# RWKV stage of a two-block layer stack: products and masks moved from GpSimd to VectorE

## The reference, cut to what matters

```python
r, k, v, gate, wd, ad = split_cols(pf, RWKV_SIZES)
w_log = -jax.nn.softplus(-(w0 + jnp.tanh(wd) @ w_up)) - 0.5
decay = jnp.exp(-jnp.exp(w_log))
a = jax.nn.sigmoid(a0 + ad @ a_up)
kk = k * k_k
k = k * (1.0 + (a - 1.0) * k_a)
kk = kk / jnp.maximum(jnp.sqrt(jnp.sum(kk * kk, axis=-1, keepdims=True)), 1e-12)
def step(S, inp):
    r_t, w_t, k_t, v_t, kk_t, a_t = inp
    sa = jnp.einsum('bhvk,bhk->bhv', S, -kk_t)
    S = (S * w_t[:, :, None, :] + sa[..., None] * (kk_t * a_t)[:, :, None, :]
         + v_t[..., None] * k_t[:, :, None, :])
    y = jnp.einsum('bhvk,bhk->bhv', S, r_t)
    return S, y
# then group norm of y over each head, y + sum(r * k * r_k) * v, times silu(gate)
```

## Time and profile before

| what | us |
|---|---|
| median of three runs (lowest, highest) | 2475.47 (2472.58, 2487.47) |
| the profiled execution | 2476.14 |
| its span, first to last instruction | 2474.3 |
| busy: PE, DVE, ACT, POOL | 2249.0, 840.2, 582.5, 585.7 |

### The profile page before, as it was taken

The page is one execution under the profiler, slowest core; times in us unless marked ns, Lnnn a source line. Parts: engine busy times, 40 slices in busy tenths (PEclk is TensorE's granted clock), DMA queues, the critical chain, the costliest instruction groups (busy, mean ns, idle before and its releaser), DMA issues.

```text
span 2474.3 us, 41370 instructions
## 1 busy us (share of the span) xinstructions
PE 2249.0 (91%) x17921; PEld 1472.3 (60%) x17921; DVE 840.2 (34%) x1741; ACT 582.5 (24%) x1209; POOL 585.7 (24%) x440
## 2 busy tenths in 40 slices
PE   8999998877789999999999979898899898889987
PEld 7888776666655568888887854433334444444442
DVE  4111315654566766223234542211221111111115
ACT  4111214442466654111123420000000000000002
POOL 5334333332111014332331321111111111111110
PEclk9999998999899999999999989999999999999999
DMA  5223211003110022221224269999999999999997
GB/s 202 85 102 128 77 70 44 12 29 121 43 58 32 1 89 97 79 60 35 60 60 173 89 230 428 430 429 429 429 428 428 431 428 429 429 429 429 428 430 292
DMA packets 73948, 538.38 MB, mean 218 GB/s; under 512 B 14152, under 2 KB 16456, under 8 KB 48032
## 3 DMA queue, kind: packets, MB, share of 16 engines
q1 hardware_dynamic: 58464, 507.55, 49.9%
q0 software_dynamic: 10240, 16.82, 1.8%
q10 hardware_dynamic: 5056, 11.28, 1.5%
HBM read 502.55 MB, written 43.52 MB: 221 GB/s over the span
## 4 chain that ended last, share of the span: by engine, by line
PE 42%; DMA 18%; DVE 3%; issue 1%; ACT 1%; DVEq 0%; POOLq 0%; ACTq 0%
PE banks L226 22%; DMA arena<-in_wg 17%; PE banks L231 6%; PE banks L233 6%; PE banks L232 6%; DMA arena<-in_wu 1%; PE banks L3185 1%; DVE arena L3489 0%; DVE arena L3479 0%; DVE arena L3329 0%; DVE wo_low L2106 0%; ACT arena L3291 0%; PE banks L1990 0%; PE banks L2814 0%; DMA arena<-in_wo 0%
## 5 line engine op out<-in xcount | busy, mean ns | idle before, releaser
L226 PE MATMUL banks<-arena 64*64 64x64 f32 (+10 forms) x13593 | 1369.8, 349 | 157.6 <-DMA arena<-in_wg 54.9
L226 PEld LDWEIGHTS banks<-arena 64*64 64x64 f32 (+4 forms) x13593 | 743.4, 152 | 722.6 <-issue 620.9
L236 ACT ACTIVATE arena<-banks 128x512 f32<-128x512 f32 (+5 forms) x357 | 195.1, 557 | 891.5 <-PE banks L226 532.7
L3179 POOL DMA_INDIRECT yb<-arena x64 | 65.0, 1016 | 789.1 <-DVE arena L3299 739.1
L3299 DVE TENSOR_SCALAR arena<-banks,arena 128x512 f32<-128x512 f32 x64 | 48.1, 751 | 503.7 <-PE banks L226 503.7
L231 PE MATMUL banks<-h1h,w2s 128*128 128x512 f32 x448 | 177.3, 396 | 1.7 <-DVE h1l L2013 1.7
L233 PE MATMUL banks<-h1h,w2s 128*128 128x512 f32 x448 | 174.6, 390 | 0.0
L232 PE MATMUL banks<-h1l,w2s 128*128 128x512 f32 x448 | 174.3, 389 | 0.0
L231 PE MATMUL banks<-hh,wlo 128*128 128x512 f32 x432 | 171.6, 397 | 0.0
L233 PE MATMUL banks<-hh,wlo 128*128 128x512 f32 x432 | 169.7, 393 | 0.0
L232 PE MATMUL banks<-hl,wlo 128*128 128x512 f32 x432 | 168.3, 390 | 0.0
(11 more groups left out here) (276 smaller groups left out, 2171.6 us busy)
## 6 DMA issues: line engine op xcount, KB each, us to landing
arena<-in_wg SPq DMA_DIRECT2D x64, 2048.0 KB, 32.9
arena<-in_wd SPq DMA_DIRECT2D x64, 2048.0 KB, 31.1
arena<-in_wu SPq DMA_DIRECT2D x63, 2048.0 KB, 26.6
arena<-in_w SPq DMA_DIRECT2D x55, 512.0 KB, 3.5
spill<-arena SPq DMA_DIRECT2D x27, 512.0 KB, 2.6
arena<-spill SPq DMA_DIRECT2D x27, 512.0 KB, 5.4
arena<-in_wo SPq DMA_DIRECT2D x16, 512.0 KB, 6.7
arena<-yb SPq DMA_DIRECT2D x8, 1024.0 KB, 13.2
```

Source lines behind the costliest of these rows:

```text
L226: return pe.e.matmul(o, l, r, start=start, stop=stop)
L236: return act.e.activation(o, i, ACT.Copy)
L3179: return pool.e.indirect_dma_start(yb, bass.IndirectOffsetOnAxis(ap=six[:, col:col + 1].bitcast(U32), axis=0), src[:, :], None, bounds_che ...
```

## The change

VectorE takes over the five products of the preparation and the three instructions of each half's front. GpSimd keeps the small product of line 839 and the tail's addition. Nothing is removed or added in sum. The diff:

```diff
@@ -787,6 +787,10 @@
         dve.wait_ge(s("rmask"), 2)
         dve.e.tensor_tensor_scan(Dn[i % 2][:, :], rmask[:, :], E1[:, :], 0.0, ALU.mult, ALU.add).then_inc(s("cum").sem, 1)
         yield
+        dve.wait_ge(s("cum"), i + 1)
+        dve.wait_ge(s("B"), i)
+        dve.wait_ge(s("K"), i)
+        dve.e.tensor_tensor(E6[:, :], Dn[i % 2][:, :], E1[:, :], ALU.subtract).then_inc(s("cum_before").sem, 1)
         yield
         for n in range(2):
             u = ps[("kk", i), "sum", n]
@@ -797,6 +801,9 @@
         dve.wait_ge(s("k_mod"), i + 1)
         dve.e.scalar_tensor_tensor(kq[:, :], E5_, 1.0, kq[:, :], ALU.add, ALU.mult).then_inc(s("k").sem, 1)
         yield
+        dve.wait_ge(s("k"), i + 1)
+        dve.wait_ge(s("r_load"), 16 * (i + 1))
+        dve.e.tensor_tensor(E5_, rq[:, :], kq[:, :], ALU.mult).then_inc(s("rk").sem, 1)
         dve.wait_ge(s("kk_scale"), i + 1)
         dve.e.scalar_tensor_tensor(E4[:, :], AR[i % 2][:, 0, :], 1e12, E4[:, :], ALU.min, ALU.mult).then_inc(s("kk_normed").sem, 1)
         yield
@@ -808,6 +815,8 @@
             dve.wait_ge(w.full, w.v)
             dve.e.tensor_tensor(E5_[:, n * 512:(n + 1) * 512], v[:, n * 512:(n + 1) * 512], u.t[:, :], ALU.mult).then_inc(u.free.sem, 1)
         yield
+        dve.wait_ge(s("kk_normed"), i + 1)
+        dve.e.tensor_tensor(E2[:, :], E2[:, :], E4[:, :], ALU.mult).then_inc(s("b").sem, 1)
         yield
         dve.wait_ge(s("exp_before"), i + 1)
         dve.wait_ge(s("kk_normed"), i + 1)
@@ -821,43 +830,21 @@
         dve.wait_ge(s("b"), i + 1)
         dve.e.tensor_tensor(Bt[i % 2][:, :], E2[:, :], E6[:, :], ALU.mult).then_inc(s("B").sem, 1)
         yield
+        dve.e.tensor_tensor(Kt[i % 2][:, :], kq[:, :], E6[:, :], ALU.mult).then_inc(s("K").sem, 1)
+        yield
+        pcb = E1[:, 63:T:64].unsqueeze(2).to_broadcast([128, 16, 64])
+        dve.e.tensor_tensor(chunks16(Dn[i % 2][:, :]), C("id2", 0, 64).unsqueeze(1).to_broadcast([128, 16, 64]), pcb,
+                            ALU.mult).then_inc(s("D").sem, 1)
         yield
 
     def pool_prologue(pool, i):
-        yield
-        yield
-        yield
-        pool.wait_ge(s("cum"), i + 1)
-        pool.wait_ge(s("B"), i)
-        pool.wait_ge(s("K"), i)
-        pool.e.tensor_tensor(E6[:, :], Dn[i % 2][:, :], E1[:, :], ALU.subtract).then_inc(s("cum_before").sem, 1)
-        yield
-        yield
+        for _ in range(5):
+            yield
         if i:
             u = ps["bonus", i - 1, 1]
             pool.wait_ge(u.full, u.v)
         pool.e.tensor_scalar(rkb[:, :], C("blk"), P("rk", i), None, ALU.mult).then_inc(s("rk_rows").sem, 1)
-        pool.wait_ge(s("k"), i + 1)
-        pool.wait_ge(s("r_load"), 16 * (i + 1))
-        pool.e.tensor_tensor(E5_of(i), rq[:, :], kq[:, :], ALU.mult).then_inc(s("rk").sem, 1)
-        yield
-        yield
-        pool.wait_ge(s("kk_normed"), i + 1)
-        pool.e.tensor_tensor(E2[:, :], E2[:, :], E4[:, :], ALU.mult).then_inc(s("b").sem, 1)
-        yield
-        yield
-        yield
-        wait_main(pool, i - 2)
-        pool.wait_ge(s("exp_minus"), i + 1)
-        pool.e.tensor_tensor(Kt[i % 2][:, :], kq[:, :], E6[:, :], ALU.mult).then_inc(s("K").sem, 1)
-        yield
-        pcb = E1[:, 63:T:64].unsqueeze(2).to_broadcast([128, 16, 64])
-        pool.wait_ge(s("exp_cum"), i + 1)
-        pool.e.tensor_tensor(chunks16(Dn[i % 2][:, :]), C("id2", 0, 64).unsqueeze(1).to_broadcast([128, 16, 64]), pcb,
-                             ALU.mult).then_inc(s("D").sem, 1)
-        yield
-
-
+        yield
 
     def tokens(hf, jj, p):
         at = (4 * hf + jj) * 128 + 64 * p
@@ -1119,11 +1106,21 @@
                                     u.t[:, :].rearrange("p (h j n) -> p h j n", h=2, j=2), sc, ALU.mult).then_inc(u.free.sem, 1)
                 if g == 0:
                     yield
+            id2 = C("id2", 0, 64).unsqueeze(1)
+            dve.wait_ge(u.free, u.v)
+            A = SC[:, :, :, 0, :].rearrange("p h j n -> p (h j) n")
+            dve.e.tensor_tensor(A, A, id2.to_broadcast([128, 8, 64]), ALU.add).then_inc(s("A_first").sem, 1)
             u = ps["AB", i, hf]
             dve.wait_ge(u.full, u.v)
             m1 = C("m1", 0, 64).unsqueeze(1).unsqueeze(1).to_broadcast([128, 2, 4, 64])
             dve.e.tensor_tensor(TTm[:, :, 0:4, :], two(u)[:, :, 0:256].rearrange("p h (j n) -> p h j n", j=4), m1,
                                 ALU.mult).then_inc(u.free.sem, 1)
+            dve.wait_ge(u.free, u.v)
+            dve.e.tensor_tensor(TTm[:, :, 0:4, :], TTm[:, :, 0:4, :], id2.unsqueeze(1).to_broadcast([128, 2, 4, 64]),
+                                ALU.add).then_inc(s("T_first").sem, 1)
+            dve.wait_ge(s("A_first"), 2 * i + hf + 1)
+            dve.e.tensor_tensor(TTm[:, :, 4:8, :], SC[:, :, :, 0, :], C("m1t", 0, 64).unsqueeze(1).unsqueeze(1).to_broadcast(
+                [128, 2, 4, 64]), ALU.mult).then_inc(s("TT_first").sem, 1)
             yield
             yield
             yield
@@ -1157,25 +1154,8 @@
             yield
 
     def pool_main(pool, i):
-        for hf in range(2):
-            wait_half(pool, i, hf)
-            yield
-            id2 = C("id2", 0, 64).unsqueeze(1)
-            u = ps["score", i, hf, 1]
-            pool.wait_ge(u.free, u.v)
-            A = SC[:, :, :, 0, :].rearrange("p h j n -> p (h j) n")
-            pool.e.tensor_tensor(A, A, id2.to_broadcast([128, 8, 64]), ALU.add).then_inc(s("A_first").sem, 1)
-            u = ps["AB", i, hf]
-            pool.wait_ge(u.free, u.v)
-            pool.e.tensor_tensor(TTm[:, :, 0:4, :], TTm[:, :, 0:4, :], id2.unsqueeze(1).to_broadcast([128, 2, 4, 64]),
-                                 ALU.add).then_inc(s("T_first").sem, 1)
-            yield
-            pool.wait_ge(s("A_first"), 2 * i + hf + 1)
-            pool.e.tensor_tensor(TTm[:, :, 4:8, :], SC[:, :, :, 0, :], C("m1t", 0, 64).unsqueeze(1).unsqueeze(1).to_broadcast(
-                [128, 2, 4, 64]), ALU.mult).then_inc(s("TT_first").sem, 1)
-            for _ in range(16):
-                yield
-
+        for _ in range(36):
+            yield
 
     def pe_tail(pe, i):
         ring = "side" if i < NP - 1 else "last"
```

## The result

The changed kernel takes **2483.7 us** (median of 20 runs, 2475.6 to 2492.2); the kernel before took 2476.55 beside it (20 runs). The ratio is 1.0023, 95% interval 1.0012 to 1.0033: 3 to 8 us slower, 5.7 in the middle, where 1.4 us faster was forecast. The time lies 0.7 us above the range. The profiled execution took 2483.8 us (span 2482.0).

The account below looks back on a forecast made before the run. The RWKV stage was taken as bound by hand-overs between engines, its change going straight to the total. Terms -4.6 + 2.2 + 1.0 = -1.4 us from the profiled 2476.1 gave 2474.7 us, range 2466 to 2483.

Parts of the forecast that it names:

- Second halves, pairs 0 to 2 (-5.5): Second score product to level 1 falls from 9.0 us to 6.69 in pair 0, 7.39 in pairs 1 and 2.
- rival 3: TensorE was not waiting for GpSimd, so the second halves give nothing: 2480 us, 8%.
- First halves: 0: Pairs 0 to 2: VectorE's identities and TT end before line 748 frees TensorE's bank, margin 0.6 us, so no cost.
- r k (+2.2): First halves: product ahead of line 801 and level 4's masking costs 1.0, 0.6 and 0.6 us in pairs 0 to 2.
- K (+0.9): Second halves, pairs 0 to 2: product before level 1's copy exposes 0.3 us beyond VectorE's 0.83 us wait, three times.
- b and E6 (0): First halves: b behind the bonus and E6's 1.22 us difference both fall into VectorE's waits, costing 0.
- D (0): End of a pair: 1.14 us ahead of the next first score product, hidden by later waits, so 0.
- Pair 3, second half (+1.0): Three more VectorE instructions add 2.07 us before level 0; a product no longer stretched gives back 1.0.
- The clock (0): TensorE's clock falls behind idles, but a shorter idle was given no extra gain from it.
- the equal 9.0 us: Second score product to level 1 took 8.96, 9.00 and 8.97 us before, the same at either clock level.
- Rival 1: VectorE's queue becomes the bound; E6's difference, D and the rest of K are exposed: 2484 us, 12%.
- Rival 2: TensorE's clock stays up in the stretches that ran at 0.50: 2467 us, 10%.

Follow-up runs that it names:

- 10: Changed kernel with K and D of pairs 1 to 3 later, normed kk one round later, identities and TT back on GpSimd: 2467.9 us, ratio to before 0.9963.
- 5: Changed kernel with identities and TT one round later, K and D of pairs 1 to 3 later, normed kk one round later: 2462.5 us, ratio to before 0.9942.
- 11: Changed kernel with only the next pair's loads of k and r started later, behind the second half's qG product: 2477.2 us, ratio to before 1.0000.
- 1: Changed kernel with the two identities and TT one round later, behind the state additions on VectorE: 2475.1 us, ratio to before 1.0003.
- 12: Changed kernel with identities and TT one round later and the loads of k and r later, K and D in place: 2467.8 us, ratio to before 0.9970.
- 6: Changed kernel with identities and TT one round later, K and D of pairs 1 to 3 behind level 4: 2468.2 us, ratio to before 0.9969.
- 3: Kernel before with only the five preparation products on VectorE, identities and TT still on GpSimd: 2477.9 us, ratio to before 1.0005.
- 14: Changed kernel with identities and TT later, normed kk later and loads of k and r later, K and D in place: 2462.0 us, ratio to before 0.9937.
- 4: Changed kernel with K and D of pairs 1 to 3 moved behind level 4 of the second half: 2475.1 us, ratio to before 0.9990.
- 13: Kernel before with only the loads of k and r started later, behind the second half's qG product: 2472.4 us, ratio to before 0.9980.

## Why the prediction was wrong

- **Second halves, pairs 0 to 2 (-5.5): the chain was right.** It was 6.25, 6.8 and 7.0 us, and the front's move is worth 5.2 us where nothing else stands in its way (10 against 5). That the waits of 2.51 us go with it and come back in 10 takes out rival 3. In after itself only pairs 1 and 2 show the gain. Pair 0's second half is 1 to 4 us longer, with the stop of 1.82 us and the low clock behind it; with the loads late (11) it takes 29.7 us.
- **First halves: 0, with a margin of 0.6 us: the step that failed.** I asked when the front would end and who waits for it, and found level 0, covered by line 748. That was right (1). I did not ask what stands behind the front in VectorE's list. The additions do, and TensorE waits for these ahead of level 0: 12.9 us of such waits in the stage instead of 0.8, 6.8 of them in first halves. They take back what the second halves gave. Putting the front behind the additions gave back 5 us; this moves it in second halves too, and what share the additions have in the 5 us is not shown. In pair 3 the front was said to be covered by an "issue" wait of 3.39 us. That held: an addition held TensorE 2.58 us, but the 3.39 were gone, and TensorE came from the transposes behind its scores (lines 955, before 968) to the same block of 126 matmuls in 11.8 us (11.3 in the second profile), 13.4 and 13.6 before. In second halves I priced the additions as time between the front's instructions (0.35 a pair), not as work that became late.
- **r k (+2.2), K (+0.9), b and E6 (0): right within what was measured**, as the products alone cost 1.2 us (-1.5 to 4.2). E6 went where forecast: VectorE's wait of 1.64 us became 0.50. The step itself of r k is 2.3 us, 2.36 forecast (VectorE, pair 0):

```profile
385.49 1.22 DVE L806 TENSOR_TENSOR arena<-arena 128x1024 f32<-128x1024 f32 x1
386.62 1.22 DVE L808 SCALAR_TENSOR_TENSOR arena<-arena 128x1024 f32<-128x1024 f32 x1
387.76 0.75 DVE L1135 TENSOR_TENSOR arena<-banks,arena 128x256 f32<-128x256 f32 x2
```

- **D (0): not separable from zero in the time** (12 against 6), though in pair 1 VectorE no longer waits at the second score and TensorE waits 0.53 us there; in pair 2 VectorE's wait of 2.12 us became 1.02, as forecast.
- **Pair 3, second half (+1.0):** +1.0 in the first profiles, +3.4 in the second ones; an addition behind the front holds TensorE 2.84 us there, 0.79 before.
- **The clock (0):** weighed, and put at nothing for the equal 9.0 us. In the profiles the stage is longer by slower matmuls, 4 to 12 us, and not by standing; this term, too, was not nothing there.
- **The rivals.** Rival 1 gave 2484, close to the 2483.7, but by another mechanism: E6, D and K exposed. Kernels 3 and 12 take that away, so the match is luck. The half of it that was right is where it decides: in first halves, by VectorE's strict order. Rival 2 needed more than one closed gap: the clock rose to 0.84 from 409 to 418, and behind the stop of 1.82 us it was low from 422 on instead. The rule of the Trainium skill ("TensorE: Matmul & The Clock Gate", section "HAM oscillation — how this bites in real kernels") fits in direction: where the state waits are 1.3 to 2.8 us and no load stands in the way, in 6, 12, 14 and 5, the stage's clock is 0.93, 0.94, 0.95 and 0.97. That the stops alone make the difference is not shown.

With the 5 us of kernel 1 in place of 0 the sum is -1.4 + 5.0 = +3.6 us, inside the measured 3 to 8; kernel 1 itself, the change without the failed step, is at +0.7 (-1.5 to 3.2), and the sum without that step was -1.4.

## What to carry to other kernels

When instructions move to an in-order engine, look behind them as well as ahead: list what they now delay, and who waits for that, down to the one 0.2 us addition that frees a buffer. A round later in the same list can take a loss away, so the place is part of the change. And follow what a moved instruction releases: a product's end may start a load that costs more than the product does. Last, count TensorE's standing and the time of its matmuls apart: a change can leave the first as it was and still lengthen the second.

## What the runs showed of the hardware

- Behind two loads of 512 KB each, at about 178 GB/s over six microseconds, TensorE stopped for 1.8 us without any semaphore (1.82, 1.81, 1.88 and 1.86 us in after, its second profile, 1 and 3), against 0.30 to 0.57 at the same place in six profiles with the loads elsewhere (4, 5, 6, 10, 13, 14) and 0.30 and 0.54 in the two of before, where they end over 5 us before TensorE gets so far. The Trainium skill, "Runtime: NRT & Kernel Launch", section "Instruction fetch mechanics", says that each engine fetches its instructions by DMA, mostly hidden. The traces agree, and show where it was not hidden: in the four stops the packet of the instruction queue started 0.2 to 0.3 us before the loads' last packet ended, and TensorE went on 1.29 to 1.45 us after the packet's end.
- A 512-column product on VectorE went from 0.68 to 2.86 us beside one GpSimd product of 2.34 us, and ended 0.54 us after it.
- The same kernel's half took 35.3 and 32.8 us in two profiles; 1.7 us of that is one run of 224 matmuls, at 0.67 and at 1.00.
